# A dense gate array filled by accumulating indirect DMAs instead of one-hot matmuls, in a two-layer gated-branch decoder step

## What is computed

```python
q = (xb @ w_query).reshape(PEER_BLOCK, PEER_HEADS, 2, D_KEY_HALF)
s = jnp.einsum('thpk,hpnk->thpn', q, sub_keys)
s_top, i_top = lax.top_k(s, PEER_TOPK)                       # 16 of 128, for each half
cand = s_top[:, :, 0, :, None] + s_top[:, :, 1, None, :]     # 16 x 16 sums
best, pos = lax.top_k(cand.reshape(PEER_BLOCK, PEER_HEADS, PEER_TOPK * PEER_TOPK), PEER_TOPK)
idx = jnp.take_along_axis(cand_idx, pos, axis=-1)            # expert = 128 i + j
g = jax.nn.softmax(best, axis=-1)
a = jax.nn.gelu(jnp.einsum('td,thkd->thk', xb, expert_u[idx]))
return jnp.einsum('thk,thkd->td', g * a, expert_v[idx])
```

## Time and profile before

| | |
|---|---|
| Runs | 4553.11, 4555.05, 4564.49 us (median 4555.05) |
| Profiled execution | 4563.61 us, its span 4561.9 us |
| Busy in the span | PE 92%, DVE 60%, ACT 30%, POOL 22% |
| Mean granted TensorE clock | 0.957 |
| DMA moved | 781.05 MB, mean 171 GB/s |

### The profile page before, as it was taken

How to read it: one execution, slowest core, us unless ns; L and a number is a source line. 1 busy time by engine, 2 the same in 40 slices (tenths; PEclk the granted TensorE clock), 3 DMA queues, 4 the chain that set the end, 5 groups by cost and what they waited for, 6 DMA issues and landing times.

```text
span 4561.9 us, 79318 instructions
## 1 busy us (share of the span) xinstructions
PE 4175.1 (92%) x29440; PEld 3955.6 (87%) x29440; DVE 2733.5 (60%) x4371; ACT 1363.1 (30%) x2001; POOL 1019.5 (22%) x793
## 2 busy tenths in 40 slices
PE   4997998899999998899959979888999999999997
PEld 1786898899999998899927768888999999998997
DVE  1256547966766435677722475478667664376776
ACT  2221323233333332233222113233333333322332
POOL 0045000000122116742200530000001221378321
PEclk8998999999999998999979989999999999999998
DMA  4243221354454566899633322214444446588994
GB/s 141 101 112 105 85 79 62 101 162 139 133 186 169 182 199 243 289 350 352 254 107 125 107 89 93 74 61 129 145 134 149 169 168 211 187 301 296 361 346 154
DMA packets 304236, 781.05 MB, mean 171 GB/s; under 512 B 36352, under 2 KB 159616, under 8 KB 301488
## 3 DMA queue, kind: packets, MB, share of 16 engines
q1 hardware_dynamic: 187344, 483.65, 32.0%
q10 hardware_dynamic: 69600, 154.15, 9.3%
q0 software_dynamic: 47104, 141.00, 9.0%
HBM read 655.79 MB, written 122.88 MB: 171 GB/s over the span
## 4 chain that ended last, share of the span: by engine, by line
PE 74%; DVE 10%; issue 6%; DMA 3%; POOL 3%; ACT 2%; another core or an unknown queue 1%; SPq 0%; DVEq 0%; ACTq 0%; POOLq 0%
PE pg L1317 15%; PE pg L1320 15%; PE pg L1318 15%; PE pm L1352 4%; PE pm L1526 4%; PE pg L1565 3%; DMA raw<-stream 3%; PE pm L1567 3%; PE pm L1566 3%; PE pg L1566 3%; PE pg L1567 3%; PE pm L1565 3%; DVE ys L1000 2%; POOL hid_pick L503 2%; DVE w_lo L841 1%
## 5 line engine op out<-in xcount | busy, mean ns | idle before, releaser
L1317 PE MATMUL pg<-a_hi,w_hi 128*128 128x260 f32 x6400 | 1705.3, 287 | 128.5 <-DVEq L872 40.6
L1318 PE MATMUL pg<-a_lo,w_hi 128*128 128x260 f32 x6400 | 1685.3, 285 | 0.1
L841 DVE TENSOR_TENSOR w_lo<-raw,w_hi 128x1024 fp32r<-128x1024 f32 x688 | 858.9, 1250 | 1320.9 <-ACT w_hi L750 814.7
L1317 PEld LDWEIGHTS pg<-a_hi,w_hi 128*128 128x128 f32 x6400 | 1225.6, 192 | 146.5 <-issue 110.0
L1320 PE MATMUL pg<-a_hi,w_lo 128*128 128x260 f32 x6400 | 1302.2, 285 | 0.0
L1318 PEld LDWEIGHTS pg<-a_lo,w_hi 128*128 128x128 f32 x6400 | 1222.4, 191 | 0.6 <-issue 0.3
L1320 PEld LDWEIGHTS pg<-a_hi,w_lo 128*128 128x128 f32 x6400 | 999.7, 191 | 0.0
L750 ACT CAST w_hi<-raw 128x1024 fp32r<-128x1024 f32 x504 | 529.2, 1050 | 851.7 <-PE pm L1567 653.0
L499 POOL DMA_INDIRECT rows<-stream,at_v x256 | 291.3, 1138 | 865.3 <-issue 457.4
L548 ACT ACTIVATE hid<-pg 128x260 f32<-128x260 f32 x512 | 170.4, 385 | 956.7 <-PE pg L1320 953.2
L509 POOL TENSOR_TENSOR one_j<-one_j,g_lo 128x1024 fp32r<-128x1024 f32 x98 | 185.9, 1897 | 1080.9 <-DVEq L1220 1080.9
(11 more groups left out here) (221 smaller groups left out, 5883.8 us busy)
## 6 DMA issues: line engine op xcount, KB each, us to landing
raw<-stream SPq DMA_DIRECT2D x784, 512.0 KB
hidden_dram<-hid SPq DMA_DIRECT2D x256, 196.0 KB, 3.4
gate_dram<-gate_buf ACTq DMA_DIRECT2D x14, 3584.0 KB, 11.8
hid_in<-hidden_dram ACTq DMA_DIRECT2D x64, 784.0 KB
gate_in<-gate_dram ACTq DMA_DIRECT2D x64, 784.0 KB
hid_tok<-hid SPq DMA_DIRECT2D x256, 64.0 KB, 3.4
rows<-stream,at_v POOLq DMA_INDIRECT x256
hid_pick<-hid_tok,at_e POOLq DMA_INDIRECT x256
```

The source lines that it names most:

```text
L841: tt(ring(False, s), raw[:, s], ring(True, s).bitcast(F32), ALU.subtract).then_inc(lo_ready, 1)
L1317: pe.matmul(outs[h], w[0], a[h][0], start=first, stop=False)
L1318: pe.matmul(outs[h], w[0], a[h][1], start=False, stop=False)
```

## The change

The one-hot tiles, their matmuls, the transposes and `gate_buf` are gone. `gate_dram` is now laid out like `hidden_dram` (partition, expert column j, token). ACT clears it in each layer's trunk with seven DMAs of 128 x 7 x 1024 zeros (`clear_gates`), four at the four `T_U` tiles, three in the `T_C` loop. DVE turns every pick into an element address (`at_g`), and POOL adds the gates at these addresses with indirect DMAs of 128 numbers each (`put_gates`): three token tiles of 128 tokens with 128 DMAs each, and 8 DMAs for the 8 samples, whose picks go through DRAM once to stand on 128 partitions. POOL waits before each head's 16 DMAs until those of the head before have landed, since the same expert may come twice. The token tiles are cut anew: the gathered tokens are now the first 128 (before the last 128), and are routed last; the dense ones are three tiles of 128 and one of 8. The gather of the first five rows moves behind the puts. ACT waits for all puts at up block 118 and then loads the first groups, before at block 113. The DVE steps at the layer's end are split differently between the dense and the gathered tokens.

```diff
-ND = 392
-GT = T - ND
-RT_TOK, RT_N = 98, 4
-GS = 8
-GB = 56
+GT = P
+ND = T - GT
+TILES = ((GT, P), (GT + P, P), (GT + 2 * P, P), (SEQ, NS), (0, GT))
+SAMPLES, GATHERED = 3, 4
+ZEROS, ZERO_RUN = 7, 7
+PUTS = SAMPLES * TOPK + 1
-    gate_dram = nc.dram_tensor("gate_dram", (GBN, P, NBLK, GB), F32).ap()
+    gate_dram = nc.dram_tensor("gate_dram", (P, NBLK, ND), F32).ap()
+    gate_elems = gate_dram.rearrange("p j t -> (p j t)").unsqueeze(1)
...
         @block.gpsimd
+                def put_gates(h, at, gates, k):
+                    pool.indirect_dma_start(gate_elems, bass.IndirectOffsetOnAxis(ap=at[:, k:k + 1], axis=0), gates[:, k:k + 1], None,
+                                            compute_op=ALU.add).then_inc(put[h], 16)
+                pool.wait_ge(zeroed, (l + 1) * (16 * ZEROS))
+                for t in range(SAMPLES):
+                    pool.wait_ge(at_ready, l * len(TILES) + (t + 1))
+                    for h in range(HEADS):
+                        if h or t:
+                            pool.wait_ge(put[h - 1], l * (16 * PUTS) + 16 * TOPK * (t + 1 if h else t))
+                        for k in range(h * TOPK, (h + 1) * TOPK):
+                            put_gates(h, at_g[:, t, :], gate_d[:, t, :], k)
+                pool.wait_ge(turn_in, (l + 1) * 32)
+                for h in range(HEADS):
...
+                    put_gates(h, at_s, gate_s, h)
-                pool.wait_ge(at_ready, l + 1)
+                pool.wait_ge(at_ready, (l + 1) * len(TILES))
                 for k in range(ROWS):
                     gather_row(k)
-                for n in range(NSUB):
-                    one_lo(n)
...
         @block.scalar
+            def clear_gates(n):
+                act.dma_start(gate_dram.rearrange("p j t -> p (j t)")[:, n * ZERO_RUN * D:(n + 1) * ZERO_RUN * D].rearrange(
+                    "p (r d) -> p r d", d=D), zero[:, :].unsqueeze(1).to_broadcast([P, ZERO_RUN, D])).then_inc(zeroed, 16)
...
                 for c in range(BC):
                     read_product(l, T_U + c + 1, c, lambda h, c=c: ys[:, 1, c, h * HT:(h + 1) * HT], ACT.Gelu_apprx_tanh)
                     split(l, 2, c)
+                    clear_gates(c)
...
-                    elif block < G_END:
-                        take_gates(block - G_FROM)
-                    if block == G_END + 4:
-                        act.wait_ge(g_out, (l + 1) * (16 * GBN) + 1)
+                    if block == NBLK - 10:
+                        for h in range(HEADS):
+                            act.wait_ge(put[h], (l + 1) * (16 * PUTS))
                         for s in range(4):
                             act.wait_ge(hid_out[s], (l * (NBLK // 4) + 2) * 32 + 1)
                         load_group(0)
                         load_group(1)
...
-                    own.do(act.copy(score[0:RT_TOK, s % 2, 0:4, :], pm[0:RT_TOK, b, :].rearrange("p (t n) -> p t n", t=4)))
-                    own.do(act.copy(score[:, s % 2, 4, :], pm[:, b + 1, 0:P]))
+                    own.do(act.copy(score[:, s % 2, 0:SAMPLES, :], pm[:, b, 0:SAMPLES * P].rearrange("p (t n) -> p t n", t=SAMPLES)))
+                    own.do(act.copy(score[0:NS, s % 2, SAMPLES, :], pm[0:NS, b, SAMPLES * P:]))
+                    own.do(act.copy(score[:, s % 2, GATHERED, :], pm[:, b + 1, 0:P]))
...
         @block.vector
-                        for r, t in ((slice(0, RT_TOK), slice(0, RT_N)), (slice(0, P), slice(RT_N, ROUTED))):
+                        for r, t in ((slice(0, P), slice(0, SAMPLES)), (slice(0, NS), slice(SAMPLES, SAMPLES + 1)),
+                                     (slice(0, P), slice(GATHERED, GATHERED + 1))):
                             own.do(dve.tensor_copy(top_v[r, t, bass.ds(i * 4 + s, 1), :].rearrange("p t o k -> p t (o k)"), pick_v[r, s, t]))
                             own.do(dve.tensor_copy(top_i[r, t, bass.ds(i * 4 + s, 1), :].rearrange("p t o k -> p t (o k)"), pick_i[r, s, t]))
...
         @block.tensor
-                with pe.Fori(0, NSUB // 4) as i:
-                    for k in range(4):
-                        up(l, i, G_FROM + k)
-                        gates(l, i, k)
+                with pe.Fori(0, NBLK // 4) as i:
+                    for k in range(4):
+                        up(l, i, k)
```

More of the change, by code:

```diff
@@ L222, in build @@
         coef = sb(peer, "coef", [P, PICKS])
-        turned = ExitStack()
-        rt = sb(turned, "rt", [P, 3, ND])
-        hid = sb(turned, "hid", [P, 4, T])
+        at_g = sb(peer, "at_g", [P, GATHERED, PICKS], U32)
+        gate_d = sb(peer, "gate_d", [P, GATHERED, PICKS])
+        at_s = sb(peer, "at_s", [P, HEADS], U32)
+        gate_s = sb(peer, "gate_s", [P, HEADS])
+        hid = sb(peer, "hid", [P, 4, T])
         tops = ExitStack()
-        top_v = sb(tops, "top_v", [P, ROUTED, HP, TOPK])
-        top_i = sb(tops, "top_i", [P, ROUTED, HP, TOPK])
+        top_v = sb(tops, "top_v", [P, len(TILES), HP, TOPK])
+        top_i = sb(tops, "top_i", [P, len(TILES), HP, TOPK])
         qs = ExitStack()
@@ L259, in build @@
         h_lo0 = sb(down, "h_lo0", [P, 4, ND], F32R)
-        hid_in01 = sb(down, "hid_in01", [P, 2, 4, ND])
-        gate_in01 = sb(down, "gate_in01", [P, 2, GBN, 4 * GB])
+        hid_in = sb(down, "hid_in", [P, 3, 4, ND])
+        gate_in = sb(down, "gate_in", [P, 3, 4, ND])
         down.close()
[L263 to L267, removed]
         peer.close()
@@ L360, in _ @@
                 sp.sem_inc(count, 1)
-            for count in counts_from_two:
-                sp.sem_inc(count, 2)
             sp.sem_inc(row_used, ROWS)
@@ L439, in _ @@
             own.do(pool.tensor_copy(own_row[:, :], own_row_u[:, :]))
+            own.do(pool.memset(zero[:, :], 0.0))
+            own.settle()
+            for t in range(GATHERED):
+                own.do(pool.tensor_scalar(own_col[:, t:t + 1], own_row[:, :], float(t * P), None, ALU.add))
             own.settle()
@@ L804, in _ @@
-                    if block == G_END + 4:
-                        act.wait_ge(g_out, (l + 1) * (16 * GBN) + 1)
+                        if t == SAMPLES + 1 and k == 1:
+                            act.wait_ge(at_ready, l * len(TILES) + t)
+                            act.sem_inc(passed, 1)
+                            act.dma_start(turn_at, at_g[0:NS, SAMPLES, :]).then_inc(turn_out, 16)
+                            act.dma_start(turn_gate, gate_d[0:NS, SAMPLES, :]).then_inc(turn_out, 16)
+                        if t == SAMPLES + 1 and k == 4:
+                            act.wait_ge(turn_out, (l + 1) * 32)
+                            act.sem_inc(passed, 1)
+                            act.dma_start(at_s[:, :], turn_at.rearrange("s (k h) -> (s k) h", h=HEADS)).then_inc(turn_in, 16)
+                            act.dma_start(gate_s[:, :], turn_gate.rearrange("s (k h) -> (s k) h", h=HEADS)).then_inc(turn_in, 16)
@@ L1110, in tops_of @@
                     dve.sem_inc(passed, 1)
-                    tiles = [(t, slice(0, RT_TOK if t < RT_N else P)) for t in range(ROUTED)]
+                    tiles = [(t, slice(0, n)) for t, (_, n) in enumerate(TILES)]
                     for t, r in tiles:
@@ L1500, in scores @@
                     b = 2 * (s % 2)
[L1501 to L1503 removed]
+                    for t, (t0, n) in enumerate(TILES):
+                        mm = pe.matmul(pm[0:n, b + t // 4, t % 4 * P:(t % 4 + 1) * P], q_t[:, s % 2, t0:t0 + n], k, start=True, stop=True)
+                    mm.then_inc(s_prod, 1)
                 with pe.Fori(0, HP // 4) as i:
```

189 lines of the change are left out of this document (57 added, 132 removed).

## The result

The changed kernel takes 4854.9 us (median of 4 runs, 4840.6 to 4860.7) against 4559.8 for the kernel before (4553.1 to 4569.4): a ratio of 1.063, 95% interval 1.060 to 1.067. The forecast was 4405, with a range from 4372 to 4660. It is 295 us slower where 150 less were expected. The profiled execution has a span of 4854.5 us against 4561.9.

The account below looks back on a forecast made before the run. PE, busy 92% of the span, was taken to bound the kernel. One-hots -184, puts +16, clears +10, query stage +8 gave -150: 4563.6 to 4413.6, or 4405 as the runs' median; range 4372 to 4660.

Parts of the forecast that it names:

- The step that failed: POOL's puts in the up stage: no extra issue cost taken for accumulating, since direct loads showed pieces to be cheap.
- The threshold: Up stage, block 118: puts cost only where their end plus 3 us passes 1540.5, when PE's two further products are done.
- E: End of the first layer's puts on POOL, forecast at 1545 us; loss 8 us a layer, 16 in all.
- Rival C: Puts between 914 us and block 118: accumulating ones dearer than gathers, 4773 us if 0.47 more each; chance 0.24.
- break-even of 0.19 a put: Puts in the up stage: from 0.19 us more a put on, the change would be slower than the kernel before.
- One-hots out, 184: Up stage, bound by PE: removing one-hot matmuls and transposes saves 92.0 us a layer, 184 in all.
- Landing, 3.0: Puts to DRAM: each exposed landing takes 3.0 us after its issue ends, 32 exposed landings.
- by 2.0: Puts' landing at the skill's fixed cost of about 2 us: puts end some 60 us earlier, no loss at all.
- The 1.12 and 1.02 taken for the issue: POOL's issue of a put; with the 0.30 gap, 1.42 us while DVE routes and 1.32 later.
- Clears 5, copies 4 a layer: Trunk: clears delay loads, 5 us a layer, 10 in all; query stage: added top-list copies, 4 a layer, 8 in all.
- D's full backlog: Trunk: clears hold up loads by the full 47 us a layer, giving 4489 us; chance 0.06.
- A wait of over 95 us there means C: ACT's wait after up block 118: about 20 us expected; over 95 would mean accumulating puts dearer than gathers.

Follow-up runs that it names:

- plain_scatter: The changed kernel with puts that overwrite instead of adding, so shared picks lose a gate; 4442.1 us, 0.977 of the kernel before.
- few12: The changed kernel with only 12 of each head's 16 gates put, still accumulating; 0.982 of the kernel before.
- spread_late: The changed kernel with clears spread over the branch stage and ACT's wait for the puts moved from up block 118 to 123; 1.052 of the kernel before.
- few4: The changed kernel with only 4 of each head's 16 gates put, still accumulating; 4380.7 us, 0.963 of the kernel before.
- few4_spread: few4 with the seven clears issued one after every third step of the trunk's branch stage; 4361.6 us, 0.959 of the kernel before.
- presum_seq: presum with heads in order, tile by tile, each waiting until the head before it has landed; 1.006 of the kernel before.
- paced_2: presum with each head also waiting for the landing of the one two before; samples accumulate, their gates misplaced; 0.974 of the kernel before.
- presum: spread_late with DVE summing shared gates for two tiles and samples, put plain; heads of different tiles take turns; 1.095 of the kernel before.
- plain_spread_late: spread_late with plain puts instead of accumulating ones, so shared elements lose a gate; 0.967 of the kernel before.
- paced_4: paced_2 with a head waiting for the one four before it instead of two; 0.976 of the kernel before.
- best: paced_2 with the samples' gates put where they belong, all gates in place; 4433.6 us, 0.974 of the kernel before.

## Why the prediction was wrong

- *The step that failed* is the sentence "That an accumulating put costs POOL more than a gather no row shows; ... and I take nothing". It is a cost put at nothing. An accumulating put holds POOL 1.55 us, a plain one 0.96, a gather 0.94. The reason given, that pieces are cheap by the direct loads, spoke of another kind of DMA; on what an addition does to the issue there was no row. A cost without a row has no nearest value to take: it should have been bounded by something like a doubling of the gather's 0.94, and the forecast weighed with that end in it.
- *The size.* The sum put the end of the first layer's puts at 1545; it was 1780. Of the 235: POOL's issue 648 us instead of 417, +231; the start at 926 instead of 914, +12; the gaps and the last landing 206 instead of 214, -8. plain_scatter parts this by cause: its puts end at 1575, so 30 of the 235 have nothing to do with accumulation (issue 453, +36; start +12; gaps and landing 196.5, -17), and the keyword makes 205 (195 in the issue, 10 in the gaps).
- *The threshold was right*, and so was the chain E -> ACT's wait -> both buffers full -> PE idle. few12 and spread_late follow it. It also explains the size of the miss: E was forecast 8 us beyond the point from which it costs (1537.5), so nothing of an error in the price of a put was absorbed, and each of the 392 errors of 0.59 (1.65 us a put in the mean against 1.06) counted in full in both layers.
- *Rival C* was the outcome, with its mechanism and place; its example of 0.47 a put gave 4773, with 0.59 the same sum is -184 + 2 x (392 x 0.59 + 8) + 18 = +313, from 4560 to 4873 against 4855. Its break-even of 0.19 a put was well placed: a straight line between plain_scatter (0.977) and the change (1.063), an estimate, crosses 1 at 0.16. Its chance of 0.24 was too low for a term that no row bounded from above.
- *One-hots out, 184*: confirmed. The pitch is 5.753 from block 4 to 118, few4's two up stages are 182.3 shorter than before, and few4 comes out at -168 where the terms without puts give -166.
- *Landing, 3.0*: close in the mean, and by luck. After the end of issue a put lands in 2.1 to 2.6 us or in 3.9 to 4.4 (plain: 17 of 31 in 1.9 to 2.0, 11 in 3.7 to 4.4). The mean of the 31 gaps is 3.04, where 3.3 with the usual 0.30 was taken. The Trainium skill (DMA: Bandwidth & Descriptors, "Anatomy of one DMA") has a fixed cost of about 2 us. Counted from the end of issue the short rows come near it; counted from its begin, as the prediction did for its "by 2.0", a short plain put takes 2.9 and an accumulating one 3.8.
- *Contention.* The Trainium skill (SBUF — State Buffer, "Who interferes with whom") says that a DVE instruction with two SBUF inputs contends with a GpSimd instruction that reads SBUF. The trace agrees: plain puts take 1.287 us beside `w_lo`, 0.961 beside nothing. The 1.12 and 1.02 taken for the issue contain this effect (1.063 in the mean) and were 0.1 too low for plain puts (1.159), 36 us a layer.
- *Clears 5, copies 4 a layer*: 7.4 in the first layer (few4 against few4_spread) and 2.1; another 2.1 arise in the first layer's trunk with the clears spread, unexplained. The clears' landing halves when they are spread, which fits the mechanism as told, that in a row they share the DMA engines with the stream's loads. D's full backlog did not come.
- *What was to show it.* "A wait of over 95 us there means C": 238. "Wrong if a put's issue costs more than 1.1 us on average, ... or if the puts end outside 1490 to 1600": 1.646 against 1.1, and 1780. The list was right to ask for it; the number it asked for was the unknown.

## What to carry to other kernels

Before work is moved to indirect DMAs on POOL, count them and multiply by the pitch of their own kind (here 1.26 us for 128 elements plain, 1.85 accumulating, and 0.1 to 0.3 more in the mean with the DVE work of these kernels beside it). Then compare the end with the moment at which someone waits: before it they are free, after it each one costs its whole pitch. Accumulate only where two sources can meet in one element. Where puts must wait for landings, let independent groups take turns: the landings that presum_seq showed (117.6 us of waits) fell to 12.5 in paced_2. Watch the stores and loads beside them: in presum they stalled, and the cause is not known.

## What the hardware showed that was not expected

- An indirect DMA with an addition takes 0.59 us more of POOL's time for 128 elements than without (1.549 against 0.962 median, DRAM as target; 1.540 against 0.986, SBUF as target).
- Beside DVE steps that read two tiles a put takes longer than beside none: beside `w_lo` 1.287 against 0.961 us in the mean for a plain one and 1.616 against 1.548 for an accumulating one, beside steps of 128 x 2048 up to 3.1 and 3.6.
- The landing of a put has two sizes after the end of issue: 2.1 to 2.6 or 3.9 to 4.4 us with addition (the change), mostly 1.9 to 2.0 or 3.7 to 4.4 without (plain_scatter). With nothing else running the change shows only the short one. What makes the long one no view here shows.
- While 108 accumulating puts ran alone, the DMA engines were busy for 20% of 225 us. That is an estimate of 52 ns an element (0.20 x 16 x 225 us / 13,824); plain ones in presum's window and the little traffic beside them took 5% of 100 us for 79 puts, 8 ns at most.
- Seven clears of 3.6 MB one after another land in 28 us in the median, spread out in 12.7, beside the same loads.
- In presum SP's stores and loads stood still for up to 124 us at a time while DMA engines were 5% busy. All 16 of these stalls began during heads of plain puts. The number of puts in flight does not explain them, as shown above, and six kernels with plain puts on four other chips (plain_scatter; presum_seq and plain_spread_late; paced_2 and paced_4; best) have none. Which queue or memory resource stands behind them, and whether the chip decides, stays open.
